# Five address phases for the rounded weights of the five feed-forward networks

## The reference

```python
h = x + (rwkv7_time_mix(...), nsa_attention(...)) @ w_out      # first block: projection "in", output projection "out" 0
h = h + swiglu(rms_norm(h), w_gate, w_up, w_down)              # network 0 (D_FF = 2816)
x = rms_norm(h, norm_f_g)
x = x + 0.5 * swiglu_2(rmsnorm(x), ...)                        # network 1
x = x + even_mixer(...)                                        # GLA + FoX: projection "even", output projection 1
x = x + 0.5 * swiglu_2(...); x = x + 0.5 * swiglu_2(...)       # networks 2 and 3
x = x + odd_mixer(...)                                         # DSA: projection "odd", output projection 2
x = x + 0.5 * swiglu_2(...)                                    # network 4
return rmsnorm(x, final_norm_g)
```

## Time and profile before

| | before |
|---|---|
| median of three runs | 1425.08 us (1424.33 to 1425.86) |
| profiled execution, first to last instruction | 1422.4 us |
| TensorE matmuls busy | 1395.2 us (98%), 10044 instructions |
| TensorE weight loads busy | 1286.2 us (90%) |
| VectorE busy | 944.7 us (66%) |
| ScalarE busy | 691.0 us (49%) |
| GpSimd busy | 82.9 us (6%) |
| DMA | 239.47 MB, 168 GB/s over the span |
| granted TensorE clock | 0.999 of 2.4 GHz |

### The profile page before, as it was taken

One profiled execution on the slowest core, in us unless ns is written; L12 is line 12 of the kernel. 1 busy time (PEld: TensorE's weight loads), 2 busy tenths in 40 slices (PEclk: granted clock), 3 DMA queues, 4 the chain that ended last, 5 costly groups with the idle time before them and its releaser, 6 DMA issues. The chain is left out here.

```text
span 1422.4 us, 25483 instructions
## 1 busy us (share of the span) xinstructions
PE 1395.2 (98%) x10044; PEld 1286.2 (90%) x10044; DVE 944.7 (66%) x1539; ACT 691.0 (49%) x1107; POOL 82.9 (6%) x137
## 2 busy tenths in 40 slices
PE   8999999999999999999999999999999999999997
PEld 8898888999989999899989999999998988899997
DVE  5778567766668666567577666676665676676665
ACT  6764545433454443376654433444433655643342
POOL 1030010000020000000000000100000123000000
PEclk9999999999999999999999999999999999999999
DMA  9344005645526555433356545365554423465540
GB/s 359 135 160 185 2 25 228 222 177 183 197 108 228 209 184 177 178 104 133 120 207 224 189 177 182 129 229 198 194 177 178 149 90 134 177 222 180 194 158 30
DMA packets 33069, 239.47 MB, mean 168 GB/s; under 512 B 6864, under 2 KB 13280, under 8 KB 14304
## 3 DMA queue, kind: packets, MB, share of 16 engines
q1 hardware_dynamic: 30320, 234.84, 45.6%
q10 hardware_dynamic: 2672, 3.58, 0.7%
HBM read 236.15 MB, written 2.25 MB: 168 GB/s over the span
## 5 line engine op out<-in xcount | busy, mean ns | idle before, releaser
L498 PE MATMUL ps<-uT_h,w_gu 128*128 128x256 f32 x3520 | 614.1, 279 | 2.5 <-ACT uT_h L1316 2.5
L498 PEld LDWEIGHTS ps<-uT_h,w_gu 128*128 128x128 f32 x3520 | 538.0, 188 | 13.8 <-issue 5.0
L498 PE MATMUL ps<-uT_l,w_gu 128*128 128x256 f32 x1760 | 478.8, 279 | 0.0
L498 PE MATMUL ps<-w_dn,h_r 128*128 128x512 f32 x1320 | 325.7, 396 | 0.3 <-DVE h_r L2070 0.3
L498 PEld LDWEIGHTS ps<-uT_l,w_gu 128*128 128x128 f32 x1760 | 325.5, 188 | 0.0
L498 PEld LDWEIGHTS ps<-w_dn,h_r 128*128 128x128 f32 x1320 | 239.6, 188 | 51.3 <-issue 1.4
L1368 ACT CAST w_gu<-ring 128x2048 fp32r<-128x2048 f32 x110 | 210.0, 1909 | 156.2 <-PE ps L498 155.6
L2028 DVE TENSOR_TENSOR w_gu<-ring,w_gu 128x2048 fp32r<-128x2048 f32 x110 | 252.1, 2292 | 35.2 <-ACT w_gu L1368 35.2
L2061 DVE TENSOR_TENSOR us<-ps,bc 128x256 f32<-128x256 f32 x110 | 46.5, 423 | 203.2 <-PE ps L498 203.2
L1381 ACT ACTIVATE wk<-wk 128x256 f32<-128x256 f32 x110 | 46.1, 419 | 260.7 <-DVE wk L2059 260.7
L1374 ACT CAST w_dn<-ring 128x1024 fp32r<-128x1024 f32 x110 | 115.7, 1052 | 82.8 <-PE ps L498 82.7
(11 more groups left out here) (398 smaller groups left out, 1696.0 us busy)
## 6 DMA issues: line engine op xcount, KB each, us to landing
ring<-wstream SPq DMA_DIRECT2D x144, 1536.0 KB, 6.6
cst<-consts_in SPq DMA_DIRECT2D x1, 2185.0 KB, 13.7
wk<-t_row ACTq DMA_DIRECT2D x1, 2048.0 KB, 8.0
wk<-masks_in SPq DMA_DIRECT2D x1, 1216.0 KB, 24.1
x<-x_in SPq DMA_DIRECT2D x2, 512.0 KB, 4.7
ring<-wstream SPq DMA_DIRECT2D x1, 1024.0 KB, 8.8
inh<-gains ACTq DMA_DIRECT2D x2, 512.0 KB, 9.6
tri_blocks<-wk SPq DMA_DIRECT2D x3, 256.0 KB, 2.8
```

The source lines that it names most:

```text
L498: return pe.matmul(o, l, r, start=start, stop=stop, skip_group_check=True)
```

## The change

Each of the five networks gets views of its own on the two copies of its weights. FFN_AT gives the element at which network f begins: 8, 24, 40, 72, 104, that is 32, 96, 160, 288 and 416 bytes behind the start of `wk`. With `wk` at 96 modulo 512 the phase of the `w_gu` pieces to the activations becomes 0, 64, 128, 256 and 384 for networks 0 to 4. Between the four buffers of a network lie gaps of 128 elements (512 bytes), so that a network's buffer stays clear of the neighbouring buffers of the networks beside it (the shifts differ by 96 elements at most); a gap of 512 bytes leaves the phase as it is. `sg` moves up by 512 elements, which keeps its phase. Nothing else is changed: every instruction, its shape, its order and its waits stay.

```diff
+FFN_AT = [8, 24, 40, 72, 104]

-        w_gu = over("w_gu", [P, 2, 2, 2 * D], "wk")
-        w_dn = over("w_dn", [P, 2, 2, D], "wk", 8 * D)
+        w_gu = [[over(f"w_gu{2 * f + j}", [P, 2, 2 * D], "wk", FFN_AT[f] + j * (4 * D + P)) for j in range(2)]
+                for f in range(5)]
+        w_dn = [[over(f"w_dn{2 * f + j}", [P, 2, D], "wk", FFN_AT[f] + 2 * (4 * D + P) + j * (2 * D + P))
+                 for j in range(2)] for f in range(5)]

-        sg = wk[:, 12 * D:12 * D + 2 * T].rearrange("p (a b) -> p a b", a=2)
+        sg = wk[:, 12 * D + 4 * P:12 * D + 4 * P + 2 * T].rearrange("p (a b) -> p a b", a=2)

-            def gate_up(j, between=None):
+            def gate_up(f, j, between=None):
...
-                            w = w_gu[:, j % 2, a, (m * KC + k) * P:(m * KC + k + 1) * P]
+                            w = w_gu[f][j % 2][:, a, (m * KC + k) * P:(m * KC + k + 1) * P]
...
-            def first_gate_up(norm):
+            def first_gate_up(f, norm):
...
-            def down_part(j, t, half, start, stop):
+            def down_part(f, j, t, half, start, stop):
                 for n, (a, b) in enumerate(PASSES):
                     last = mm(ps[2 * t + half][:, :], h_r[:, j % 2, a, t * P:(t + 1) * P],
-                              w_dn[:, j % 2, b, half * 512:(half + 1) * 512], start and n == 0, stop and n == 2)
+                              w_dn[f][j % 2][:, b, half * 512:(half + 1) * 512], start and n == 0, stop and n == 2)
...
-                act.copy(w_gu[:, c % 2, 0, :], slot(i)[:, 0:2 * D]).then_inc(s["hi_a"], 1)
+                act.copy(w_gu[f][c % 2][:, 0, :], slot(i)[:, 0:2 * D]).then_inc(s["hi_a"], 1)
...
-                act.copy(w_dn[:, c % 2, 0, :], slot(i)[:, 2 * D:3 * D]).then_inc(s["hi_b"], 1)
+                act.copy(w_dn[f][c % 2][:, 0, :], slot(i)[:, 2 * D:3 * D]).then_inc(s["hi_b"], 1)
...
-                v.tensor_tensor(w_gu[:, c % 2, 1, :], slot(i)[:, 0:2 * D], w_gu[:, c % 2, 0, :].bitcast(F32),
+                v.tensor_tensor(w_gu[f][c % 2][:, 1, :], slot(i)[:, 0:2 * D], w_gu[f][c % 2][:, 0, :].bitcast(F32),
                                 ALU.subtract).then_inc(s["lo_a"], 1)
...
-                v.tensor_tensor(w_dn[:, c % 2, 1, :], slot(i)[:, 2 * D:3 * D], w_dn[:, c % 2, 0, :].bitcast(F32),
+                v.tensor_tensor(w_dn[f][c % 2][:, 1, :], slot(i)[:, 2 * D:3 * D], w_dn[f][c % 2][:, 0, :].bitcast(F32),
                                 ALU.subtract).then_inc(s["lo_b"], 1)
```

More of the change, by code:

```diff
@@ L567, in first_gate_up @@
                         for a in range(2):
-                            mm(ps[4 + 2 * m][:, 0:T], w_gu[:, 0, a, (m * KC + k) * P:(m * KC + k + 1) * P],
+                            mm(ps[4 + 2 * m][:, 0:T], w_gu[f][0][:, a, (m * KC + k) * P:(m * KC + k + 1) * P],
                                uT_r[0][:, k, :], k == 0 and a == 0, False)
@@ L573, in first_gate_up @@
                             pe.wait_ge(s["uT_lo"], 16 * TN[norm] + 8 + k + 1)
-                        last = mm(ps[4 + 2 * m][:, 0:T], w_gu[:, 0, 0, (m * KC + k) * P:(m * KC + k + 1) * P],
+                        last = mm(ps[4 + 2 * m][:, 0:T], w_gu[f][0][:, 0, (m * KC + k) * P:(m * KC + k + 1) * P],
                                   uT_r[1][:, k, :], False, k == KC - 1)
@@ L585, in spread_rstd, with down @@
                     mm(ps[1][0:16, 0:384], C("t5")[0:32, :], C("t5_onehot")[0:32, :]).then_inc(s["t5_ps"], 1)
-            def down_part(j, t, half, start, stop):
+            def down_part(f, j, t, half, start, stop):
                 for n, (a, b) in enumerate(PASSES):
                     last = mm(ps[2 * t + half][:, :], h_r[:, j % 2, a, t * P:(t + 1) * P],
-                              w_dn[:, j % 2, b, half * 512:(half + 1) * 512], start and n == 0, stop and n == 2)
+                              w_dn[f][j % 2][:, b, half * 512:(half + 1) * 512], start and n == 0, stop and n == 2)
                 return last
-            def down(j, start):
+            def down(f, j, start):
                 for t, half in PARTS:
-                    last = down_part(j, t, half, start, False)
+                    last = down_part(f, j, t, half, start, False)
                 last.then_inc(s["down_done"], 1)
@@ L606, in step @@
                     if c == 0:
-                        first_gate_up(norm)
+                        first_gate_up(f, norm)
                     else:
-                        gate_up(c, (lambda: spread_rstd(norm)) if c == 1 else None)
+                        gate_up(f, c, (lambda: spread_rstd(norm)) if c == 1 else None)
                     if 0 < c < FC - 1:
@@ L614, in step @@
                             pe.wait_ge(s["t5_sb"], 1)
-                        down(c - 1, c == 1)
+                        down(f, c - 1, c == 1)
                 step(0)
@@ L627, in ffn @@
                 for t, half in PARTS[0:3]:
-                    down_part(FC - 2, t, half, False, False)
+                    down_part(f, FC - 2, t, half, False, False)
                 pe.wait_ge(s["lo_b"], q + FC)
@@ L631, in ffn @@
                 for t, half in PARTS[0:3]:
-                    down_part(FC - 1, t, half, False, True).then_inc(s["acc_done"], 1)
+                    down_part(f, FC - 1, t, half, False, True).then_inc(s["acc_done"], 1)
                 first_T(n, 0)
-                down_part(FC - 2, 1, 1, False, False).then_inc(s["down_done"], 1)
-                down_part(FC - 1, 1, 1, False, True).then_inc(s["down_done"], 1)
+                down_part(f, FC - 2, 1, 1, False, False).then_inc(s["down_done"], 1)
+                down_part(f, FC - 1, 1, 1, False, True).then_inc(s["down_done"], 1)
                 first_T(n, 1)
```

## The result

The changed kernel takes 1428.91 us in the median of seven runs (1427.46 to 1429.06), the kernel before 1424.97 us in its seven. The ratio is 1.0028 with a 95% interval of 1.0018 to 1.0038: 3.9 us slower, with 1428.6 forecast. The total came out as said, and most of the way to it did not.

A forecast was written before the change was run, and what follows sets the result against it. TensorE, busy 1395.2 of 1422.4 us, was taken to bound the kernel. Network 0 added 3.5 us, networks 1 to 4 and `down` nothing: 1425.1 + 3.5 = 1428.6 us, range 1416 to 1443.

The forecast's parts named there:

- TensorE's own pace is the bound, and only it changes: Whole kernel: TensorE busy 1395.2 of 1422.4 us; a network chunk takes its 8.40 us of matmuls, which alone this change touches.
- The three paces of the trace before: Matmuls of one shape at 113.3, 116.7 and 120.0 ns, read as address effects; phase 0 at 120.0, -32 at 116.7.
- "even" is a mixture of the two: Projection "even", 117.9 ns: two of three stationary pieces at -32, the third at 0, which would give 117.8.
- Network 0: 3.5 us: Gate and up in network 0, phase -32 to 0: 1056 matmuls, 3.3 ns slower each, 3.5 us more; chance 0.33.
- `down`: nothing: The `down` matmuls in all networks: no change from shifted weights; at most 1.8 us a network either way.
- Networks 1 to 4: no change: Gate and up at phases 64, 128, 256 and 384: taken to stay at 116.7 ns, adding nothing.
- my bounds: Gate and up in networks 1 to 4: between +3.5 us (120.0 ns) and -3.6 us (113.3 ns) a network.
- C: All networks: period between 64 and 512; with 256, networks 0 and 3 slow (1432.1), with 128, 0, 2, 3, 4 (1439.2); chance 0.14.
- E: Some phase beats -32 and 0: each good network gives 3.6 us back; 1421.4 with two, 1414.2 with four; chance 0.22.
- B: Phase modulo 64 counts, so all five networks slow to 120.0 ns: 17.6 us more, 1442.7; chance 0.17.
- D: Addresses do nothing anywhere, and 120.0 ns belongs to the projection "in": 1425.1 us; chance 0.14.
- The rule: TensorE's two operands read through independent ports, so no weight address changes its pace: 1425.1 us.

## Why the prediction was right, and where it was not

- **TensorE's own pace is the bound, and only it changes.** Right. The idle time stayed (27.2 and 27.1 us), the large copy and subtraction took 1907 and 2292 ns as before (1909 and 2292), and each change in a chunk is the sum of its matmuls.
- **The three paces of the trace before are an effect of phase.** Right for 116.7 and 120.0, though it rested on a coincidence of stages. That "even" is a mixture of the two is not borne out: in the stretch of the earlier trace rows the distances behind its three passes are 118.1, 118.0 and 117.1 ns on average, none at 120.0, and with every tile at 64 "even" still had stretches at 118. The run with the other phases and the one with all tiles moved showed it: same network, other distance, other pace; same distance, other address, same pace. Phase 0 gave 120.0 ns, as the earlier trace rows had it.
- **Network 0: 3.5 us.** The right sign; the size was 2.2 us. Gate and up cost 48 x 3.1 = 0.15 us a chunk, as forecast 0.16. The other 0.05 us is the next step.
- **`down`: nothing.** Wrong. At phase 0 and 64 it is 229 ns and not 233, at 128 and 384 it is 231: 0.02 to 0.05 us a chunk back in all five networks. I had read the earlier trace rows as insensitive, but 4 ns on a third of the matmuls would be some 1.3 ns in their mean, too little to tell from other differences; at 64 the same projections went to 228.9.
- **Networks 1 to 4: no change.** This is the step that failed, as I took the middle of my bounds four times. Measured: 22 x -0.187 = -4.1 us in network 1, below the bound of -3.6 from the earlier trace rows since `down` helped, and +1.6, +2.2 and +1.6 in 2, 3 and 4. They add up to +1.3 us, and this with the 2.2 of network 0 is 3.5. So the forecast total was hit by luck, through two errors that cancelled: network 0 too dear by 1.3, the other four too cheap by 1.3.
- **The rivals.** C with a period of 256 was true for 0 and 3 (the same pace) and for 2 and 4, and E for network 1: both were on the list, as alternatives, and they held at the same time. B is out (0 and 64 differ most of the five phases), and so is D. The bounds of some ±3.5 us a network held in all but network 1, which went 0.5 below; the chances would have been better placed on a mixture.
- **The rule.** That the two operands read through ports of their own and that TensorE waits on nobody is what the Trainium skill has, page "SBUF — State Buffer", section "Who interferes with whom"; the prediction drew 1425.1 us from it. No wait for another engine does appear in the rows, so the trace contradicts only what I had drawn from the rule, that an address can do nothing: matmuls of one shape start 113.3, 116.7, 117.8 or 120.0 ns apart at full clock.

## What to carry to other kernels

If TensorE is busy throughout, compare the distances between starts from stage to stage: equal shapes at unequal paces can come from where the tiles lie. Try the distance of weights to activations in steps of 32 bytes over 256 bytes, for every kind of matmul that alternates, and read the pace of each in the trace; here it was worth 1.3% of the kernel for one constant. Then measure the whole: the kernel in which every matmul had the best distance by itself lost the pace in its networks, through distances between tiles of neighbouring matmuls. Several values in one kernel, one for each layer, make one run a survey, but its total says little.

## What was not expected of the hardware

A one-pass `float32r` matmul of 128x128 by 256 columns starts every 113.3 to 120.0 ns in these kernels (granted clock 0.996 to 0.999 of 2.4 GHz), and one of 512 columns every 228.8 to 235.2. The steady pace depends on the distance of its operands modulo 256 bytes, and on the distances to the tiles of the matmuls before. At distance 64 there are two paces, 113.3 and 117.8 ns, and what ran before chooses; one network changed from the one to the other with every chunk. At 192 the same two were seen, and at -32 116.7 and 117.9, there only in the first chunks of a network. The two kernels with this distance in the projections also scattered more from run to run (1401.98 to 1406.46 and 1419.91 to 1425.06) than the kernel before in the same sets (1423.53 to 1425.44). That the state is chosen anew in each execution would explain it; no profile of two executions of one kernel was compared, so it is only argued. The clock is a rival in part: the two slowest of the second kernel (1425.06 and 1423.38) had 0.996 granted and its others 0.998 or 0.999, though the kernel before stayed within 1424.2 to 1425.2 at 0.997. What in the memory or in TensorE makes the pattern was not tried, and stays open.
